# Value projections with 512 moving columns, gates by a tangent, and the two softmaxes of a differential head joined before their turn

## What is computed

```python
h = x @ w_in                                   # q, k, v of four branches, then four gates of width 1024
ya = forgetting_attention(...)                 # branch A, 4 heads, causal
yb = banded_attention(..., sinks)              # branch B, 4 heads, window of 128 keys
# branch C, differential: two softmaxes a head, each with 32-wide q and k, one shared v
p = softmax(q1 @ k1.T * scale + bias) - lam * softmax(q2 @ k2.T * scale + bias)
yc = p @ v
yc = yc * rsqrt(mean(yc * yc) + eps) * diff_norm_g * (1 - lam_init)
yd = dilated_attention(...)                    # branch D, 4 heads
for i, y in enumerate((ya, yb, yc, yd)):
    merged = merged + sigmoid(gates[:, :, i]) * (y @ w_branch[i])
x = layer_norm(ALPHA * x + merged @ w_out, ...)
x = layer_norm(ALPHA * x + mixture_of_experts(x), ...)
```

## Time and profile before

| what | us |
|---|---|
| median of 3 runs | 1391.29 |
| lowest, highest | 1389.23, 1391.63 |
| span of the profiled execution | 1378.4 |
| median less that span | 12.9 |
| PE busy in the span | 1311.1 (95%) |
| DVE busy | 889.9 (65%) |
| ACT busy | 709.0 (51%) |
| POOL busy | 390.4 (28%) |

### The profile page before, as it was taken

The page is one execution under the profiler, slowest core; times in us unless marked ns, Lnnn a source line. Parts: engine busy times, 40 slices in busy tenths (PEclk is TensorE's granted clock), DMA queues, the critical chain, the costliest instruction groups (busy, mean ns, idle before and its releaser), DMA issues.

```text
span 1378.4 us, 15980 instructions
## 1 busy us (share of the span) xinstructions
PE 1311.1 (95%) x6084; PEld 972.3 (71%) x6084; DVE 889.9 (65%) x1167; ACT 709.0 (51%) x863; POOL 390.4 (28%) x262
## 2 busy tenths in 40 slices
PE   7999999999979999998999999999999999999965
PEld 4989886666656677445587777777777777777732
DVE  4001115655575556465388888888888888888858
ACT  4232323333322321002278888888788888787810
POOL 3232222212233343126232323232222222233301
PEclk9999999999999999998999999999999999999988
DMA  4732201111111151504399999999999999999776
GB/s 159 257 104 75 71 20 58 59 52 43 40 56 58 58 205 51 218 5 153 136 385 372 375 368 376 371 373 368 367 366 370 369 371 367 372 371 366 284 315 250
DMA packets 68124, 311.37 MB, mean 226 GB/s; under 512 B 17788, under 2 KB 17916, under 8 KB 41552
## 3 DMA queue, kind: packets, MB, share of 16 engines
q1 hardware_dynamic: 48560, 276.64, 53.3%
q0 software_dynamic: 19488, 33.70, 6.5%
HBM read 305.74 MB, written 42.01 MB: 252 GB/s over the span
## 4 chain that ended last, share of the span: by engine, by line
PE 67%; DMA 22%; ACT 4%; DVE 3%; issue 2%; SPq 1%; POOL 0%; POOLq 0%; DVEq 0%; ACTq 0%
DMA raw<-in_w_gu 20%; PE PS L653 18%; PE PS L898 9%; PE PS L848 4%; PE PS L851 4%; PE PS L845 4%; PE PS L761 4%; PE PS L779 4%; PE PS L709 4%; ACT w_hi_e L1122 3%; PE PS L732 3%; PE PS L720 2%; DMA parts<-y_d 2%; PE PS L830 2%; PE PS L682 2%; PE PS L681 2%
## 5 line engine op out<-in xcount | busy, mean ns | idle before, releaser
L1438 DVE TENSOR_TENSOR w_lo_e<-raw,w_hi_e 128x2048 fp32r<-128x2048 f32 x192 | 433.6, 2282 | 3.1 <-ACT w_hi_e L1122 2.9
L1122 ACT ACTIVATE w_hi_e<-raw 128x2048 fp32r<-128x2048 f32 x192 | 368.5, 1920 | 111.4 <-DMA raw<-in_w_gu 71.7
L1666 POOL DMA_INDIRECT y_d<-y_slots,tab x64 | 113.6, 1775 | 424.4 <-PE PS L917 307.7
L1618 POOL TENSOR_TENSOR w_lo<-ring,w_hi 128x1024 fp32r<-128x1024 f32 x54 | 128.3, 2376 | 325.9 <-ACT w_hi L1029 325.9
L1282 DVE CUSTOM_DVE_ANT_0 region<-PS,region 128x128 f32<-128x128 f32 (+1 forms) x64 | 30.6, 477 | 183.0 <-PE PS L709 181.0
L848 PE MATMUL PS<-w_hi_e,xs_lo 128*128 128x512 f32 x512 | 144.6, 404 | 0.0
L845 PE MATMUL PS<-w_hi_e,xs_hi 128*128 128x512 f32 x512 | 143.8, 402 | 0.0
L851 PE MATMUL PS<-w_lo_e,xs_hi 128*128 128x512 f32 x512 | 138.6, 392 | 0.0
L1073 ACT ACTIVATE region<-region,nmax 128x128 f32<-128x128 f32 (+3 forms) x80 | 43.6, 545 | 150.0 <-DVE nmax L1282 149.7
L848 PEld LDWEIGHTS PS<-w_hi_e,xs_lo 128*128 128x128 f32 x512 | 91.7, 188 | 33.3 <-DVE xs_lo L1464 16.0
L851 PEld LDWEIGHTS PS<-w_lo_e,xs_hi 128*128 128x128 f32 x512 | 96.1, 188 | 22.3
(11 more groups left out here) (180 smaller groups left out, 2151.6 us busy)
## 6 DMA issues: line engine op xcount, KB each, us to landing
raw<-in_w_gu SPq DMA_DIRECT2D x128, 1024.0 KB, 11.3
raw<-in_w_down_e SPq DMA_DIRECT2D x64, 1024.0 KB, 10.8
ring<-in_w_merge SPq DMA_DIRECT2D x32, 640.0 KB, 3.8
ring<-in_w_proj SPq DMA_DIRECT2D x22, 512.0 KB, 3.7
parts<-y_d SPq DMA_DIRECT2D x8, 1024.0 KB, 16.2
parts<-y_d SPq DMA_DIRECT2D x4, 1536.0 KB, 13.1
region<-in_w_out SPq DMA_DIRECT2D x1, 4096.0 KB, 14.0
bias_d<-bias_rows SPq DMA_DIRECT2D x3, 1280.0 KB, 11.9
```

The source lines that it names most:

```text
L1122: nc.scalar.activation(w_hi_e[b][:, lo:hi], raw[b][:, lo:hi], ACT.Copy).then_inc(made, 1)
L1438: nc.vector.tensor_tensor(w_lo_e[b][:, lo:hi], raw[b][:, lo:hi], w_hi_e[b][:, lo:hi].bitcast(F32), ALU.subtract).then_inc(made, 1)
L1618: nc.gpsimd.tensor_tensor(wl, w, wh.bitcast(F32), ALU.subtract).then_inc(w_lo_made, 1)
L1666: pool.indirect_dma_start(y_d, bass.IndirectOffsetOnAxis(ap=rows, axis=0), y_slots[:, b, :], None, bounds_check=last_row, oob_is_err=False ...
```

## The change

The value projections use the same product as q and k (weights stationary, 512 token columns moving). Their result has features on the partitions, goes to `vT` (which lies where `gate` lies), and a new item `turn_v` transposes it in four 128 x 128 blocks; ACT copies these to `V`. The gate becomes 0.5 * (1 + tanh(g/2)): ACT takes the tangent, DVE does (tanh + 1) * product in one instruction in `gated`, the factor 0.5 goes into the copy of `yT`, and the items' additions and reciprocals on DVE (and `invert`) are gone. In branch C a head's steps run over the query tile outside and over c inside; at the item `turn` of the second component DVE runs `combine`, which scales the two sets of probabilities by their reciprocal sums and by lambda and adds them; then there is one turn and one value product for both, and `out_step` only copies.

```diff
-            + [(BR_C, h, c, q) for h in range(4) for c in range(2) for q in range(QT)]
+            + [(BR_C, h, c, q) for h in range(4) for q in range(QT) for c in range(2)]
...
+def has_values(s):
+
+    return STEPS[s][0] != BR_C or STEPS[s][2] == 1
...
+    order = [("proj", c) for c in range(6)] + [("turn_v", 4)]
...
-        if s >= 1:
+        if s >= 1 and has_values(s - 1):
             out.append(("turn", s - 1))
-        if s >= 2:
+        if s >= 2 and has_values(s - 2):
             out.append(("values", s - 2))
...
-            plan = [part(m, 0), 1, part(m, 1), 1, part(m, 2), 1, [("branch", m), ("invert", m)], 1,
+            plan = [part(m, 0), 1, part(m, 1), 1, part(m, 2), 1, [("branch", m)], 1,
...
-                    (x_product_tokens if PROJ[n][0] == "v" else x_product)(bank, n).then_inc(proj_done, 1)
+                    x_product(bank, n).then_inc(proj_done, 1)
...
-                    pe.wait_ge(probs_made, n + 1)
+                    if br == BR_C:
+                        pe.wait_ge(combined, (n - FIRST_C) // 2 + 1)
+                    else:
+                        pe.wait_ge(probs_made, n + 1)
...
+                elif kind == "turn_v":
+                    u = turn_at[kind, n]
+                    pe.wait_ge(proj_out, n + 1)
...
+                    for t in range(QT):
+                        mm = nc.tensor.transpose(PS[:, T_BANK + u % 2, t * P:(t + 1) * P],
+                                                 vT[:, V_AT[PROJ[n][1:]] % 2, t * P:(t + 1) * P], ident[:, :])
+                    mm.then_inc(turned, 1)
...
-                    nc.scalar.activation(gate[:, n % 2, :], PS[:, C_BANK, :], ACT.Exp, scale=-1.0)\
-                        .then_inc(gate_exp, 1)
+                    nc.scalar.activation(gate[:, n % 2, :], PS[:, C_BANK, :], ACT.Tanh, scale=0.5)\
+                        .then_inc(gate_tanh, 1)
...
+            def combine(s):
+                nk = keys_of(BR_C, STEPS[s][3])[1] * P
+                one, two = probs[:, (s - 1) % 3, 0:nk], probs[:, s % 3, 0:nk]
+                dve.wait_ge(probs_made, s + 1)
+                link(nc.vector.reciprocal(rden[:, s - 1:s + 1], den[:, s - 1:s + 1]))
+                link(nc.vector.tensor_scalar(rden[:, s:s + 1], rden[:, s:s + 1], lam_s[:, 5:6], None, ALU.mult))
+                link(nc.vector.tensor_scalar(two, two, rden[:, s:s + 1], None, ALU.mult))
+                nc.vector.scalar_tensor_tensor(two, one, rden[:, s - 1:s], two, ALU.mult, ALU.add).then_inc(combined, 1)
...
-                elif kind == "gate":
-                    dve.wait_ge(gate_exp, n + 1)
-                    g = gate[:, n % 2, :]
-                    link(nc.vector.tensor_scalar(g, g, 1.0, None, ALU.add))
-
-                    nc.vector.reciprocal(g[:, 0:SEQ // 2], g[:, 0:SEQ // 2])
-                elif kind == "invert":
-                    g = gate[:, n % 2, SEQ // 2:SEQ]
-                    link(nc.vector.reciprocal(g, g))
+                elif kind == "turn":
+                    if STEPS[n][0] == BR_C:
+                        combine(n)
...
-                    nc.vector.tensor_tensor(dst, PS[:, C_BANK + 1, :], gate[:, n % 2, :], ALU.mult)\
+                    nc.vector.scalar_tensor_tensor(dst, gate[:, n % 2, :], 1.0, PS[:, C_BANK + 1, :], ALU.add, ALU.mult)\
```

More of the change, by code:

```diff
@@ L125, in merge @@
     def merge(m):
-        return part(m, 0) + part(m, 1) + part(m, 2), [("branch", m), ("invert", m), ("gated", m)]
+        return part(m, 0) + part(m, 1) + part(m, 2), [("branch", m), ("gated", m)]
     for s in range(16):
-        order += [("proj", proj.pop(0))] + step(s)
+        n = proj.pop(0)
+        order += [("proj", n)] + step(s) + [("turn_v", m) for m in (5 if s == 0 else n,) if PROJ[m][0] == "v"]
     for s in range(16, 20):
@@ L136, in order_of_work @@
         if STEPS[at][0] == BR_C:
-            plan = [part(m, 0), 1, part(m, 1), 1, part(m, 2), 1, [("branch", m), ("invert", m)], 1,
+            plan = [part(m, 0), 1, part(m, 1), 1, part(m, 2), 1, [("branch", m)], 1,
                     [("gated", m)]]
         else:
-            plan = [part(m, 0) + part(m, 1), 1, part(m, 2) + [("branch", m)], 1, [("invert", m), ("gated", m)]]
+            plan = [part(m, 0) + part(m, 1), 1, part(m, 2) + [("branch", m)], 1, [("gated", m)]]
         for x in plan:
@@ L182, in build @@
     order = order_of_work()
-    turns = [x for x in order if x[0] in ("turn", "turn_y")]
+    turns = [x for x in order if x[0] in ("turn", "turn_y", "turn_v")]
     turn_at = {x: n for n, x in enumerate(turns)}
@@ L381, in build @@
         probs_made = sem("probs_made")
+        combined = sem("combined")
         turned = sem("turned")
@@ L670, in x_product @@
                 return mm
[L672 to L683, removed]
             for kind, n in order:
@@ L725, in _ @@
                     k0, nk = keys_of(br, qt)
[L726 removed]
                     need = max(m for m, x in enumerate(PROJ) if x[1] == br and x[0] == "v")
[L728 to L730 removed]
+                    pe.wait_ge(turned_out, max(turn_at["turn", n], turn_at["turn_v", need]) + 1)
+                    v = VALUE_AT[n]
+                    if v >= 2:
+                        pe.wait_ge(y_made, v - 1)
                     for j in range(nk):
[L732 removed]
+                        mm = nc.tensor.matmul(PS[:, O_BANK + v % 2, 0:HD], probsT[:, v % 3, j * P:(j + 1) * P],
                                               v_of(n, k0 + j), start=(j == 0), stop=(j == nk - 1))
@@ L1054, in _ @@
                     if what == "v":
-                        nc.scalar.activation(V[:, :, V_AT[br, j], :], bank.rearrange("p (t n) -> p t n", t=QT),
-                                             ACT.Copy).then_inc(proj_out, 1)
+                        nc.scalar.activation(vT[:, V_AT[br, j] % 2, :], bank, ACT.Copy).then_inc(proj_out, 1)
                     elif br == BR_A:
@@ L1079, in _ @@
                     act.wait_ge(turned, u + 1)
-                    if n >= 3:
-                        act.wait_ge(values_done, n - 2)
-                    nc.scalar.activation(probsT[:, n % 3, 0:nk], PS[:, T_BANK + u % 2, 0:nk], ACT.Copy)\
+                    v = VALUE_AT[n]
+                    if v >= 3:
+                        act.wait_ge(values_done, v - 2)
+                    nc.scalar.activation(probsT[:, v % 3, 0:nk], PS[:, T_BANK + u % 2, 0:nk], ACT.Copy)\
+                        .then_inc(turned_out, 1)
+                elif kind == "turn_v":
+                    u = turn_at[kind, n]
+                    act.wait_ge(turned, u + 1)
+                    nc.scalar.activation(V[:, :, V_AT[PROJ[n][1:]], :],
+                                         PS[:, T_BANK + u % 2, :].rearrange("p (t n) -> p t n", t=QT), ACT.Copy)\
                         .then_inc(turned_out, 1)
@@ L1089, in _ @@
                         act.wait_ge(branch_done, (br - 1) * KT)
-                    nc.scalar.activation(yT[:, (br % 2) * 2 + j, :], PS[:, T_BANK + u % 2, :], ACT.Copy)\
+                    nc.scalar.activation(yT[:, (br % 2) * 2 + j, :], PS[:, T_BANK + u % 2, :], ACT.Copy, scale=0.5)\
                         .then_inc(turned_out, 1)
@@ L1275, in bias_step @@
                 dve.wait_ge(scores_done, s + 1)
-                if s >= 3:
+                if s >= 3 and has_values(s - 3):
                     turn_wait(s - 3)
```

35 lines of the change are left out of this document (20 added, 15 removed).

## The result

The changed kernel takes **1425.45 us** (median of 4 runs, 1422.75 to 1427.82) where the kernel before takes 1391.46 on the same chip: a ratio of 1.024 with a 95% interval of 1.0216 to 1.0264. It is 34 us slower, and the forecast was 9 us faster.

A forecast was written before the change was run, and what follows sets the result against it. PE was taken to bound nearly the whole attention, DVE counting only where PE waits. The terms -32.4 - 14.3 + 32.0 - 6.5 + 11.9 = -9.3 us from 1391.3 gave 1382 us, range 1368 to 1391.

The forecast's parts named there:

- value tiles: Value projections: seven tiles take 36.5 us less of PE, their added transposes 4.1 us more, net 32.4 us less.
- turns and value products of branch C: Branch C: 10 instead of 20 tiles a head turned and multiplied, 14.3 us of PE less.
- waits for `combine`: Branch C: PE stands still at the turn of each of 16 pairs, 1.6 to 2.3 us, 32 us more.
- gates and the waits behind them: Branch B's and last `turn_y`, branch C's norm: waits of 1.9, 2.2, 0.7 us and 1.7 of clock go, 6.5 less.
- falls of the clock: Branch C: PE's granted clock falls behind seven of the sixteen new pauses, at 1.7 us each, 12 us more.
- The twelve of 2.0 us and more: Branch C's longer new pauses of PE for `combine`, behind which the clock may fall.
- the four short ones: Branch C's new pauses of 1.6 us, behind which the clock would hardly fall.
- the second rival: Branch C: the clock falls at each pause, sixteen falls cost 27 us, 1397 us in all; chance 0.12.
- The dense parts of 1.90 us beside the pauses: Branch C: dense parts on both sides of most pauses, given as support for the clock hardly falling.
- The first rival: Branch C: the clock hardly falls, two falls, 1366 to 1374 us; chance 0.27.
- The price of a fall: Branch C: each fall of PE's clock behind a pause costs 1.7 us.
- The span: Whole kernel: the profiled execution's 1378.4 us span, with 12.9 us around it, is the median of 1391.3.

The follow-up runs named there:

- e7: The kernel before with only the value projections changed, its old gates and both components apart: 1345.82 us, ratio 0.974 to the kernel before.
- e6: The change with `combine` ahead of the next scores' bias step and the turn and values moved later: 1325.08 us, ratio 0.9598 to the kernel before.
- e1: The change without the joined softmax, value tiles and gates kept as changed: 1339.96 us, ratio 0.9709 to the kernel before.
- e2: The change with 8 to 16 unread products on PE between the scores and the wait for the joined set: 1371.88 us, ratio 0.9942.
- f1: The change as it is, run once more on a third chip: 1425.77 us, ratio 1.0228 to the kernel before.
- e3: The change with POOL's low-part subtraction cut to one column for the eight merges in branch C: 1382.08 us, ratio 1.0013 to the kernel before.
- f3: The change with four unread filling products on PE in each pause and POOL's whole subtraction: 1400.45 us, ratio 1.0062 to the kernel before.

## Why the prediction was wrong, step by step

| step | forecast, us | measured, us | from |
|---|---|---|---|
| value tiles | -32.4 | -35.9 | e7; 34.1 in the trace |
| turns and value products of branch C | -14.3 | -15 | e6 against e1 |
| waits for `combine` | +32.0 | +45.6 | the list of waits; 30.9 without POOL's subtraction |
| gates and the waits behind them | -6.5 | -4 (0 to -8) | e1 against e7 |
| falls of the clock | +11.9 | +41 (37 to 45) | e2 against the change |
| sum | -9.3 | +32 | measured in all: +34 and +32 (f1) |

Two steps failed, and the way from -9.3 to +34 us is 43 us. Some 31 of them come with POOL's subtraction, which the waits for `combine` left out (the change at 1.024, e3 at 1.0013). The other 11 or 12 are there without it (e3 stands at +1.8 us): the clock's 25 us where the forecast had 11.9, less some 2 us on the other terms.

**The falls of the clock** failed at this place: "The twelve of 2.0 us and more may fall, the four short ones hardly; I take seven falls of sixteen". With pauses as long as forecast 13 of 16 were followed by a low clock (e3), at 2 us each in the mean where I had 1.7; in the change all 16 were. That is the second rival, which had a chance of 0.12; it needs 13 falls to come out slower, and e3, which has its waits and its falls, came out within 0.13%. I had one pause with a fall, of 1.9 us, and one without, of 1.7 us, and read the difference as one between short and dense matmuls around them. The runs show another reading of these two: pauses of 1.0 us or less had no fall behind them, those of 1.56 us had one in two of four cases, and of those of 1.89 us and more all but one. The dense parts of 1.90 us beside the pauses, from which I took hope, held nothing up.

The first rival rested on the same hope, and the second rival's mechanism was the one that held. The Trainium skill ("TensorE: Matmul & The Clock Gate", section "A second HAM failure mode: psum-queue depth-cycling") has the same: where pauses between groups of matmuls are frequent the clock swings, and each swing has its cost. The traces agree for pauses of 1.89 us and more (11 of 12 in e3) and not for those of 1.0 us and less (none of seven in f3).

The price of a fall was right for the short falls and wrong for the rest. In the change, again in windows of 1 us, nine low stretches take 1.7 us each, one lasts 14 us, and three last 22 us. Each of these four begins in the pause of 3.9 us of a head, and the three of 22 us reach over the next pause too. The same four stand in f1. A short one, what follows it, a long one, and what follows that:

```profile
241.00:245.00 4.00, 3.85 (x6) 1.31 (x7) 0.10 (x1) 0.28 (x1) 0.00 (x0) 0.57 0.00 0
245.00:249.00 4.00, 4.00 (x22) 2.85 (x21) 1.18 (x4) 1.57 (x4) 0.00 (x0) 1.00 0.53 168
...
261.00:283.00 22.00, 17.61 (x43) 10.66 (x44) 5.92 (x14) 2.51 (x8) 1.44 (x1) 0.53 0.09 30
283.00:289.00 6.00, 3.17 (x16) 2.14 (x15) 2.91 (x7) 2.49 (x6) 1.80 (x1) 1.00 0.00 0
```

So a low clock did not always end with the few microseconds of work behind the pause, and the sum had no term for that.

**The waits for `combine`** were worked out right for DVE by itself, and had no term for POOL. Its four instructions took, undisturbed, 30.9 us with the bias step for a forecast of 32; single rows are 287 to 486 ns for the first product (forecast 300 to 510) and 351 to 750 for the second (350 to 750). But I asked of POOL only whether it could follow with the weights, not whether it and DVE would be in each other's way. The trace of before had the sign, at its line 1319, a product of two sets in SBUF. What it says of this line (ns least, median, most), and POOL's row in the timeline within it:

```profile
L1319 DVE SCALAR_TENSOR_TENSOR region<-region,yc_ss,norm_g x16: 272/274/2441, 398.2 to 404.2; 128x64 f32<-128x64 f32 x16
```

```profile
400.72 2.45 POOL L1618 TENSOR_TENSOR w_lo<-ring,w_hi 128x1024 fp32r<-128x1024 f32 x1 [1.48 <-ACT w_hi L1029]
```

Half of these 16 took 274 ns or less. The 2441 ns are among the five that start between 400.4 and 403.4 us, which is where POOL's 2.45 us lie. In the change two pauses a head became 3.6 and 3.9 us, outside the 1.5 to 2.7 that the prediction allowed, and longer pauses also cost more clock: 41 us for 16 are 2.6 each, against 2.0 and 2.2 in e3 and f3. Waits and clock together, the subtraction is worth 31 us, nearly all of the way from "no change" to 2.4% slower.

**The value tiles** came within 11%, with 34.1 to 35.9 us for a forecast of 32.4. By the rates of the Trainium skill ("TensorE: Matmul & The Clock Gate", section "Back-to-back issue gap"), about 81 and 131 ns a matmul, the net gain would have been 28.3 us, an estimate from those two rates. The tiles took 5.49 us, 229 ns a matmul of 512 columns, so the rows gave the better figure.

**The gates** did in the changed kernel what was forecast: 1.9, 2.5 and 0.7 us of waits went and 0.2 came, 4.9 in all for a forecast of 4.8, besides the clock behind the first. Their price on the chip, 4.3 us, was measured in a kernel without joining, and its interval holds the 6.5.

**The span.** I set 12.9 us "around" the span against the median. That was wrong too: runs lie 1.7 us above their span (1426.67 and 1425.0), and the rest is the difference between chips, on which the same kernel took 1381 and 1391 us. It did no harm, because the sum was one of differences.

The remaining misfit, 2 us in the sum, is within the intervals. That a fall costs 2.0 us in the mean in e3 and 2.6 in the change fits the long low stretches above. What keeps the clock low over 14 to 22 us in these, and why one of the pauses of over 1.89 us had no fall, stays open.

## What to carry to other kernels

A new wait of PE has two prices, its length and what the clock takes back behind it; where it comes every few microseconds the second can be the larger, so a joined or shortened piece of work must first be placed where its product is ready before PE asks. The same change was 2.4% slower with the joined set in one place of the order and 4% faster with it in another; without joining it was 2.9% faster. Ask of each DVE instruction with both inputs in SBUF that is put on the path of PE what POOL does at that moment, above all where one event starts both.

## What the hardware showed that was not expected

- A DVE tensor_scalar with a scalar from memory, 384 columns, took 2065 ns beside a POOL subtraction of 2.34 us and 422 ns without it; a scalar_tensor_tensor of 128 columns 2366 and 351. The DVE instruction ends with POOL's or up to 0.25 us behind it.
- The granted clock behind a pause of PE between blocks of work of some 6 to 12 us: 1.00 behind all seven pauses of 0.76 to 1.0 us (f3), 0.50 to 0.66 in the 4 us behind all but one of those of 1.89 us and more (11 of 12 in e3, 8 of 8 in f3, 16 of 16 in the change, where three stood in a stretch that was low already).
- How long the clock stays low differs. In the change nine low stretches were over within 5 us, three lasted 22 us with a clock of 0.53.
- Products that nobody reads made the kernel 41 us faster (e2), by keeping PE at work while it waited.
